# Two-layer hybrid decoder with hierarchical MoE: the last two experts' rows spread over tokens by TensorE, down weights loaded as blocks of 128 full rows

## The reference

```python
coarse_prob = softmax(xt @ wc + bc)            # 4 groups, the best one is taken
e_logit, e_idx = top_k(fine_sel, 2)            # 2 of the 4 experts of that group
e_w = softmax(e_logit) * g_prob
gate, up = split(xt @ w_gate_up[e])            # 1024 -> 2 x 256, 16 experts
y_e = (silu(gate) * up) @ w_down[e]            # 256 -> 1024
x = x + sum over the token's two experts of e_w * y_e
```

## Time and profile before

| | us |
|---|---|
| median of 3 runs (1177.66 to 1183.61) | 1181.36 |
| the profiled execution | 1181.09 |
| its span, from the first to the last instruction | 1179.3 |
| PE busy in the span | 1111.8 |
| DVE, ACT, POOL busy | 701.5, 608.6, 405.1 |

### The profile page before, as it was taken

One profiled execution on the slowest core, in us unless ns is written; L12 is line 12 of the kernel. 1 busy time (PEld: TensorE's weight loads), 2 busy tenths in 40 slices (PEclk: granted clock), 3 DMA queues, 4 the chain that ended last, 5 costly groups with the idle time before them and its releaser, 6 DMA issues.

```text
span 1179.3 us, 19724 instructions
## 1 busy us (share of the span) xinstructions
PE 1111.8 (94%) x7062; PEld 912.1 (77%) x7063; DVE 701.5 (59%) x1016; ACT 608.6 (52%) x903; POOL 405.1 (34%) x344
## 2 busy tenths in 40 slices
PE   8999999999998899998999999999999997999980
PEld 5778887778787688886788888888888886888870
DVE  5435444367736999996646341543442138999975
ACT  5556234242434699995633342233342234899871
POOL 4343121110133244442155325442244442344442
PEclk8999999999999899999999999999999997999995
DMA  9333311112225699996443213331222364999955
GB/s 262 79 86 56 72 38 55 37 44 66 72 68 210 244 353 375 379 364 238 174 128 98 81 56 106 97 106 56 81 73 91 104 190 161 354 388 374 358 208 223
DMA packets 89859, 194.76 MB, mean 165 GB/s; under 512 B 20348, under 2 KB 21432, under 8 KB 89016
## 3 DMA queue, kind: packets, MB, share of 16 engines
q1 hardware_dynamic: 67560, 159.34, 40.6%
q10 hardware_dynamic: 12432, 17.60, 4.4%
q0 software_dynamic: 9792, 16.80, 3.8%
HBM read 189.50 MB, written 23.07 MB: 180 GB/s over the span
## 4 chain that ended last, share of the span: by engine, by line
PE 80%; DVE 8%; DMA 5%; ACT 3%; issue 2%; ACTq 1%; SPq 0%; POOL 0%; POOLq 0%; DVEq 0%
PE ps L674 23%; PE ps L676 22%; PE ps L675 22%; PE ps L2570 2%; PE ps L2362 2%; DMA raw<-in_moe_w_down_dram 1%; DMA arena<-y 1%; DVE x L1467 1%; PE ps L2245 1%; ACTq L1421 1%; PE ps L2498 1%; DMA arena<-hs,slot_rows 1%; PE ps L2199 1%; ACT wh L1007 1%; DMA y<-arena,cur_rows 1%
## 5 line engine op out<-in xcount | busy, mean ns | idle before, releaser
L841 POOL TENSOR_TENSOR wl<-raw,wh 128x1024 fp32r<-128x1024 f32 x94 | 228.6, 2440 | 380.5 <-ACT wh L1007 380.2
L674 PE MATMUL ps<-wh,hT_hi 128*128 128x512 f32 x864 | 346.7, 401 | 3.5 <-DVE hT_lo L1986 2.4
L676 PE MATMUL ps<-wh,hT_lo 128*128 128x512 f32 x864 | 337.9, 391 | 0.0
L675 PE MATMUL ps<-wl,hT_hi 128*128 128x512 f32 x864 | 337.2, 390 | 0.0
L1007 ACT ACTIVATE wh<-raw 128x1024 fp32r<-128x1024 f32 x116 | 122.4, 1068 | 212.6 <-PE ps L676 191.0
L674 PEld LDWEIGHTS ps<-wh,hT_hi 128*128 128x128 f32 x864 | 162.8, 188 | 39.1 <-issue 3.5
L676 PEld LDWEIGHTS ps<-wh,hT_lo 128*128 128x128 f32 x864 | 162.3, 188 | 34.6
L675 PEld LDWEIGHTS ps<-wl,hT_hi 128*128 128x128 f32 x864 | 162.8, 188 | 30.9
L674 PE MATMUL ps<-hT_hi,wh 128*128 128x512 f32 (+1 forms) x296 | 116.9, 395 | 2.1 <-DVE arena_rounded L1818 1.0
L1961 DVE TENSOR_TENSOR wl<-arena,wh 128x1024 fp32r<-128x1024 f32 x96 | 113.8, 1222 | 4.7 <-ACT wh L1294 3.1
L1961 DVE TENSOR_TENSOR wl<-raw,wh 128x1024 fp32r<-128x1024 f32 x92 | 109.5, 1223 | 8.2 <-ACT wh L1294 5.4
(11 more groups left out here) (331 smaller groups left out, 1576.8 us busy)
## 6 DMA issues: line engine op xcount, KB each, us to landing
raw<-in_moe_w_gate_up_dram SPq DMA_DIRECT2D x64, 512.0 KB, 11.5
arena<-in_moe_w_gate_up_dram SPq DMA_DIRECT2D x64, 512.0 KB, 10.5
raw<-in_odd_w_in_dram SPq DMA_DIRECT2D x48, 512.0 KB, 3.7
raw<-in_even_w_in_dram SPq DMA_DIRECT2D x32, 512.0 KB, 4.8
arena<-in_moe_w_down_dram SPq DMA_DIRECT2D x32, 512.0 KB, 11.7
raw<-in_moe_w_down_dram SPq DMA_DIRECT2D x32, 512.0 KB, 14.1
raw<-in_odd_w_out_dram SPq DMA_DIRECT2D x16, 512.0 KB, 3.6
arena<-y ACTq DMA_DIRECT2D x6, 1024.0 KB, 9.9
```

The costliest lines, as they stand in the source:

```text
L674: nc.tensor.matmul(dst, lh, rh, start=first, stop=False)
L675: nc.tensor.matmul(dst, lh, rl, start=False, stop=False)
L676: return nc.tensor.matmul(dst, ll, rh, start=False, stop=last)
L841: pool.tensor_tensor(columns_of(i, wl[:, i % NSPL, :, :]), raw_columns(i), columns_of(i, wh[:, i % NSPL, :, :]).bitcast(F32), ALU.subtract ...
```

## The change

The last two experts of a layer, 14 and 15, are no longer scattered to DRAM. Their 128 rows each are evicted times the weight of the pair in each slot, and split into a high part (ACT, `late_hi`) and a low part (DVE, `late_low`). DVE builds for each of the two experts a matrix of zeros and ones, slot by token (`slot_tokens`), and PE multiplies it with the rows (`late_rows`): eight matmuls for each tile of 128 tokens, whose sum lands in two PSUM banks and is added to `X` by DVE (`add_late`). The weights of the slots go through DRAM: ACT stores `w12` in the turn of expert 1 and POOL gathers 128 values for each of the two experts.

The rows of the other fourteen experts are read as before, but by SP, as soon as the scatters of experts 12 and 13 have landed (`load_early_rows`), behind the four loads of block 10. A pair of experts 14 or 15 now has a row in `y2_dram` that nobody writes in this layer; its weight is set to zero (`w_early`), and the one `y2_dram`, which both layers now use, is cleared once near the start of the program from 512 zeros in SBUF.

In layer 0 the PE work without a result goes; the low parts of block 10 move from DVE to POOL, and two of its high parts stand before the eviction of expert 15 on ACT. A down piece is now a block of 128 weight rows with all 1,024 columns; so PE makes both halves of an expert's output with the first piece and then with the second, and half 0 is ready three matmuls before half 1 (`y_half`). ACT makes the next high part before both evictions instead of between them. Buffers of the rows move to other places of SBUF. The overflow part is changed to fit and isn't shown.

```diff
 def lo_by_dve(i):
-    return i in DVE_LO or any(m + 2 <= i < m + 6 * NE for m in MOE_PIECE) or first_piece(10) <= i < first_piece(10) + 4
...
+        w_dram = [nc.dram_tensor(f"w{l}", (2 * SEQ, 1), F32, kind="Internal").ap() for l in range(2)]
+        y2_dram = [nc.dram_tensor("y2", (2 * SEQ, DM), F32, kind="Internal").ap()] * 2
...
+        LAST = NE - 2
+        YP = [reg(at, 2048).rearrange("p (j d) -> p j d", j=2) for at in (0, 2048, 4096, 14336)]
+        no_rows = reg(21760, 512)
+        late_hi, late_lo = v3(rounded(9216, 2048), 2), v3(rounded(7168, 2048), 2)
...
-        def down_src(l, e, hf):
-            w = a["moe_w_down"][l].rearrange("e (k p) c -> p e k c", p=P)
-            c = 512 * hf
-            return w[:, bass.ds(e, 1), :, c:c + 512].squeeze(1) if not isinstance(e, int) else w[:, e, :, c:c + 512]
+        def down_src(l, e, k):
+            w = a["moe_w_down"][l].rearrange("e (k p) (h c) -> p e k h c", p=P, h=2)
+            return w[:, bass.ds(e, 1), k, :, :].squeeze(1) if not isinstance(e, int) else w[:, e, k, :, :]
...
+            def load_early_rows(l):
+
+                for q in range(2):
+                    sp.wait_ge(s_(f"y_stored{q}"), 112 * (l + 1))
+                src = y2_dram[l].rearrange("(T p j) d -> T p j d", p=P, j=2)
+                sp.dma_start(YP[0][:, 0, :], src[0][:, 0, :]).then_inc(s_("yp_loaded0"), 16)
+                sp.dma_start(YP[0][:, 1, :], src[0][:, 1, :]).then_inc(s_("yp_second0"), 16)
+                for T in range(1, NT):
+                    sp.dma_start(YP[T], src[T]).then_inc(s_(f"yp_loaded{T}"), 16)
...
             after = MOE_PIECE[0] + 6 * NE
             for i in range(after, after + 4):
                 load(i)
+            load_early_rows(0)
             overflow_sp(sp, 0)
-            sp.wait_ge(s_("yp_loaded3"), 16)
...
+            load_early_rows(1)
...
+                def late_experts():
+
+                    pool.wait_ge(s_("w_stored"), 16 * (l + 1))
+                    for e in range(2):
+                        rows = idx[:, 1, LAST + e:LAST + e + 1].bitcast(U32)
+                        pool.indirect_dma_start(out=w_slot[:, e:e + 1], out_offset=None, in_=w_dram[l],
+                                                in_offset=bass.IndirectOffsetOnAxis(ap=rows, axis=0),
+                                                bounds_check=last_pair_row, oob_is_err=False).then_inc(s_("late_ready"), 16)
+
                 two_experts(0)
-                with pool.Fori(1, NE // 2 - 1) as it:
+                two_experts(1)
+                late_experts()
+                with pool.Fori(2, NE // 2 - 2) as it:
                     two_experts(it)
                 for par in range(2):
-                    scatter(NE // 2 - 1, par, 32 * l + 31 + par)
-                    if par == 0:
-                        free_last(NE // 2 - 1, par)
+                    scatter(NE // 2 - 2, par, 28 * l + 27 + par)
...
                         hi_in(7)
+                    if not last:
+                        hi_in(8)
+                    if last and par == 1:
+                        hi(m + 6 * NE)
+                        hi(m + 6 * NE + 1)
                     act.wait_ge(s_("ysb_free"), E + 1)
+                    if last:
+                        act.wait_ge(s_("late_ready"), 32 * (l + 1))
                     for hf in range(2):
-                        act.wait_ge(used, it * 12 + (6 * NE * l + 6 * par + 4 + n0 + hf + 1))
-                        act.activation(ysb[:, par, 512 * hf:512 * hf + 512], ps[:, 2 + hf, :], ACT.Copy).then_inc(s_("y_read"), 1)
-                        if hf == 0 and not last:
-                            hi_in(8)
+                        c = slice(512 * hf, 512 * hf + 512)
+                        if hf == 0:
+                            act.wait_ge(s_("y_half"), E + 1)
+                        else:
+                            act.wait_ge(used, it * 12 + (6 * NE * l + 6 * par + 4 + n0 + 2))
+                        if last:
+                            act.activation(late_hi[:, par, c], ps[:, 2 + hf, :], ACT.Copy, scale=w_slot[:, par:par + 1]).then_inc(s_("y_read"), 1)
+                            continue
+                        act.activation(ysb[:, par, c], ps[:, 2 + hf, :], ACT.Copy).then_inc(s_("y_read"), 1)
 
                 for n in range(4):
                     expert(*divmod(n, 2))
+                    if n == 1:
+                        act.wait_ge(s_("w_ready"), l + 1)
+                        with nc.allow_non_contiguous_dma(reason="two weights of a token"):
+                            act.dma_start(w_dram[l].rearrange("(T p j) o -> p T (j o)", p=P, j=2), v3(w12, 4)).then_inc(s_("w_stored"), 16)
                 with act.Fori(2, NE // 2 - 1) as it:
                     for par in range(2):
                         expert(it, par)
...
-                for i in range(4):
+                for i in range(2, 4):
...
-                act.wait_ge(s_("y_all_stored"), l + 1)
-                for q in range(2):
-                    act.wait_ge(s_(f"y_stored{q}"), 128 * (l + 1))
-                src = y2_dram[l].rearrange("(T p j) d -> T p j d", p=P, j=2)
-                act.dma_start(YP[:, 0, 0, :], src[0][:, 0, :]).then_inc(s_("yp_loaded0"), 16)
-                act.dma_start(YP[:, 0, 1, :], src[0][:, 1, :]).then_inc(s_("yp_second0"), 16)
-                for T in range(1, NT):
-                    act.dma_start(YP[:, T, :, :], src[T]).then_inc(s_(f"yp_loaded{T}"), 16)
...
+                    if step[1] == 4:
+                        act.wait_ge(s_("y_cleared"), 16)
                     if not BLOCKS[step[1]][0].endswith("out"):
                         evac(step[1])
+                    if step[1] == 1:
+                        act.wait_ge(s_("no_rows_set"), 1)
+                        act.dma_start(y2_dram[0].rearrange("(p n) (k c) -> p (n k) c", p=P, c=512), no_rows.unsqueeze(1).broadcast_to([P, 16, 512]))\
+                            .then_inc(s_("y_cleared"), 16)
...
 
                 dve.wait_ge(s_("yp_second0" if T == 0 and j == 1 else f"yp_loaded{T}"), 16 * (l + 1))
-                D(stt(X[:, T, :], YP[:, T, j, :], w12[:, 2 * T + j:2 * T + j + 1], X[:, T, :], ALU.mult, ALU.add),
-                  s_(f"moe_added{l}") if j == 1 else None)
+                D(stt(X[:, T, :], YP[T][:, j, :], w_early[:, 2 * T + j:2 * T + j + 1], X[:, T, :], ALU.mult, ALU.add))
+
+            def late_low(l, e, hf):
+
+                c = slice(512 * hf, 512 * hf + 512)
+                dve.wait_ge(s_("late_ready"), 32 * (l + 1))
+                dve.wait_ge(s_("y_read"), 32 * l + 31 + 2 * e + hf)
+                stt(late_lo[:, e, c], ps[:, 2 + hf, :], w_slot[:, e:e + 1], late_hi[:, e, c].bitcast(F32), ALU.mult, ALU.subtract)\
+                    .then_inc(s_("late_low_made"), 1)
+
+            def add_late(l, T):
+
+                dve.wait_ge(s_("late_rows"), 4 * l + T + 1)
+                b = late_banks(l, T)
+                D(tt(v3(X[:, T, :], 2), v3(X[:, T, :], 2), ps[:, b:b + 2, :], ALU.add), s_(f"moe_added{l}"))
 
             def norm(n):
+                if n in (2, 4):
+                    l = n // 2 - 1
+                    combine(l, 0, 0)
+                    late_low(l, 1, 0)
+                    late_low(l, 1, 1)
+                    combine(l, 0, 1)
+                    add_late(l, 0)
+                    combine(l, 1, 0)
+                    combine(l, 1, 1)
+                    add_late(l, 1)
                 if n == 2:
-                    for i in range(4):
-                        lo(first_piece(10) + i)
-                    combine(0, 0, 0)
-                    combine(0, 0, 1)
-                    combine(0, 1, 0)
-                    combine(0, 1, 1)
                     dve.wait_ge(s_("wb_loaded"), 32)
-                    for T in range(NT):
+                    lo_tiles(("hT", n, 0), 0)
+                    for T in range(1, NT):
+                        if T + 1 < NT:
+                            combine(0, T + 1, 0)
+                            combine(0, T + 1, 1)
+                            add_late(0, T + 1)
                         lo_tiles(("hT", n, T), T)
-                        if T + 2 < NT:
-                            combine(0, T + 2, 0)
-                            combine(0, T + 2, 1)
                     return
                 if n == 4:
                     def last(T):
                         dve.wait_ge(s_("norm_r"), 16 + T + 1)
                         D(stt(fin(T), X[:, T, :], rs[:, T:T + 1], wb(4), ALU.mult, ALU.mult), s_("fin_dve"))
 
-                    for T in range(NT):
+                    dve.wait_ge(s_("wb_loaded"), 64)
+                    for T in (2, 3):
                         for j in range(2):
                             combine(1, T, j)
-                        if T == 2:
-                            dve.wait_ge(s_("wb_loaded"), 64)
-                            last(0)
-                    last(1)
+                        add_late(1, T)
```

(56 more changed lines are left out.)

100 lines of the change are left out of this document (61 added, 39 removed).

## The result

The changed kernel takes 1186.02 us (median of 8 runs, 1185.05 to 1187.07) against 1181.23 for the kernel before (8 runs as well): a ratio of 1.0045 with a 95% interval of 1.0031 to 1.0059. It is slower; 1175.2 was forecast, and the range ended at 1182. The profiled execution took 1186.38 us, its span is 1184.5 (before 1179.3).

The account below looks back on a forecast made before the run. TensorE, with 80% of the span, was taken as the bound, waiting at two seams after each layer's last expert. Terms -3.4 - 2.4 + 0.2 + 0.3 - 0.6 = -5.9 from 1181.09 gave 1175.2 us, range 1170 to 1182.

Parts of the forecast that it names:

- Splits moved: Block 10's four low parts go from VectorE to GpSimd, 9.8 us ending before block 10 starts; cost 0.
- seam 0: Stretch from layer 0's last expert to the end of block 10, where TensorE waits for rows; forecast -3.4 us.
- Weights of slots: Loops: ScalarE's store of 512 pairs, 0.4 us to issue and mostly absorbed by idle time; +0.3 for both layers.
- Down weights as full rows: Loops: larger DMA pieces save some 0.1 us an expert, buying only layer 1's 0.63 us stall; -0.6.
- Rows loaded early: Both layer ends: y loads wait for expert 13's scatter; first half tile lands in 5.7 us, VectorE starts at 547.3.
- rival (c): Rows land 2 to 3 us late behind block 10's weights, or VectorE's new operations hit upper bounds: 1179; chance 0.14.
- Slot matrices: Both layer ends: VectorE's six slot_tokens operations, between 1.4 and 4.1 us, taken as 2.2.
- Filler removed: TensorE without its resultless matmuls: one fall of the clock near 550 for about 3 us, costing 1.3.
- Rival (b): Clock stays down in seam 0, still 0.50 when block 10 starts, costing about 7.7 instead of 1.3: 1183; chance 0.11.
- Seam 1 summed: From layer 1's last expert to the end: last tile summed at 1167.4 instead of 1170.32; less 0.5 for clock, -2.4.
- Experts 14 and 15: End of each loop: TensorE's second half of expert 15 waits for expert 14's late_low, +0.1 a layer, +0.2.
- Clearing y once: Near 57 us, before the first loop: writing 4.2 MB is hidden by loads kept ahead; 0, at most some 2.

Follow-up runs that it names:

- run 9: Changed kernel with GpSimd making only 8 of the 1,024 columns of block 10's four low parts, the rest left out: 1175.65 us, ratio 0.9963.
- run 1: Changed kernel with block 10's four low parts made by VectorE again, ahead of layer 0's first combine: 1182.12 us, ratio 1.0026.
- run 2: Changed kernel with GpSimd starting block 10's low parts only once layer 0's slot matrices are complete: 1182.03 us, ratio 1.0017.
- run 5: Changed kernel with four extra 128x1024 GpSimd subtractions in layer 1, begun as VectorE begins the slot matrices; nothing uses their result: 1192.61 us, ratio 1.0090.
- run 6: Changed kernel with low parts on VectorE again and 27 filler calls (54 matmuls) on TensorE before layer 0's spreading: 1185.84 us, ratio 1.0035.
- run 10: Changed kernel with low parts on VectorE again and 13 filler calls (26 matmuls) on TensorE before layer 0's spreading: 1181.05 us, ratio 1.0004.
- run 3: Changed kernel without the store of pair weights and GpSimd's two gathers, rows of experts 14 and 15 weighted by 0.5: 1181.89 us, ratio 1.0011.
- run 7: Changed kernel with pair weights stored as one 32-byte run per partition instead of four 8-byte runs, plus five small VectorE steps: 1182.41 us, ratio 1.0010.
- run 11: Changed kernel with 32-byte weight store, low parts split up on VectorE, TensorE's products ahead of the next tile's transposes, and filler: 1179.58 us, ratio 0.9991.
- run 12: Changed kernel with 32-byte store, low parts spread on VectorE, its splits not waiting for each other, original TensorE order, filler: 1173.21 us, ratio 0.9949.
- run 4: Kernel before with the full-row down weights alone: 1180.38 us, ratio 1.0012.

## Why the prediction was wrong

The step that failed is in *Splits moved*: four low parts "from VectorE (4.6 us, hidden then) to GpSimd: 4 x 2.44 = 9.8", "Cost 0". I asked who waits for the low parts, and found nobody; I did not ask what VectorE does while GpSimd makes them. They cost seam 0 8.95 us (52.16 against 43.21 in run 9): 8.4 in the slot matrices, which took 10.6 us and not 2.2, and 0.45 in a longer wait for spread rows (1.04 against 0.59). Where VectorE makes them itself they cost 5.15 (run 1, 48.36). So neither engine makes them free any more: what had covered them was VectorE's wait for rows, and the change removes that wait. The Trainium skill, SBUF — State Buffer, "Who interferes with whom", says that a VectorE instruction with both inputs in SBUF contends with a GpSimd instruction that reads SBUF, that the pair of ports which the two engines share is an exclusive lock, and that an instruction with at most one SBUF input, outside the two-port modes, is not touched. The trace agrees: 2.27 us for 0.17 with two SBUF inputs (L2033), and 1.22 for 1.22 with one of two from PSUM (`add_late` in run 2). Two slow steps (L2032, and L2035 in run 5) have a single input from SBUF; the Trainium skill counts their form among those that can run in a two-port mode, and no run shows in which they ran. The exclusion lay in the trace of before too, in rows that the prediction does not use (a VectorE step of 64x16, twice, and GpSimd's low part of that time):

```profile
L1617 DVE SCALAR_TENSOR_TENSOR small<-small x2: 167/1266/2364, 92.2 to 92.4; 64x16 f32<-64x16 f32 x2
```

```profile
92.31 2.38 POOL L841 TENSOR_TENSOR wl<-raw,wh 128x1024 fp32r<-128x1024 f32 x1
```

The same step took 167 ns once and 2,364 ns beside a low part of 2.38 us. A group whose longest instance is fourteen times its shortest is worth a question.

The prediction named three signs of being wrong. Two came: the first combine is behind 550 (557.96), and the loop's 9.35 us an expert changed. The third, a fallen clock at block 10's start, did not.

The other steps:

- *Weights of slots*, +0.3: wrong. ScalarE's issue took 0.38, as taken, but the price is on the DMA engines: in the seven kernels with the 512 small pieces and no other edit in the loop (after, runs 1, 2, 5, 6, 9 and 10) the loops take 141.4 and 141.6 us on the mean, against 140.1 in both without them (run 3). That is 1.3 and 1.5 us, 2.8 in all; single loops of the seven lie between 140.5 and 142.6. (Why run 3's turns take 9.37 us and those of runs 7, 11 and 12 only 9.33 stays open; by the latter the store costs up to 0.5 a layer more.) I had bounded the issue from both sides and not the transfer, in a loop whose DMA share I had just read as 0.98.
- *Down weights as full rows*, -0.6: right by itself (-0.9 in run 4), but the store took the slack and the stalls came back.
- *Rows loaded early*: right. In run 9 SyncE issued the first half tile at 545.52; it landed 6.0 us later, against 5.7 in the earlier trace rows, and the combine started at 551.65, 6.1 us after the issue. The rows stood in SyncE's queue behind block 10's four loads, issued 1.7 to 5.8 us ahead of them, and landed behind them (the last load at 549.3): so far the trace agrees with the rule on ring order that the prediction cites from the Trainium skill (DMA: Bandwidth & Descriptors, "Queues, rings and completion order"). But the delay of 2 to 3 us by which rival (c) would have moved the sum is not seen: in the twelve profiles with this order the half tile took 5.5 to 7.0 us.
- *Slot matrices* 2.2, *spreading*, sums of 1.3: right; 2.2 in runs 1, 2 and 9, and `add_late` 1.22.
- *Filler removed*, 1.3: right in size, somewhat high. The clock fell to 0.50 for 13.7 us and not 3, since TensorE also waited for the slot matrices; it cost 1.0 us (runs 1 and 10), and in seam 1, where 0.5 was forecast, 0.8 between the profiles of either kind. Rival (b) had it stay down into block 10 and give 1183: the time came out on its side, but not by its mechanism, since the clock was back at 2.4 GHz before block 10 started. The rule of the Trainium skill cited there (TensorE: Matmul & The Clock Gate, Part 1) is borne out so far that TensorE without work fell to 1.2 GHz; the price is what waits for it.
- *Seam 1 summed*, -2.4: right, -2.7, and step by step (3.7 for 3.9 and 19.2 for 18.9). There GpSimd has no low parts to make.
- *Experts 14 and 15*, +0.2: right in size. The last turn of a loop takes 8.40 us in both layers, before 8.29 and 8.25; which wait makes it longer is not shown.
- +0.8 ahead of the first loop is not explained; over all the profiled runs this stretch lies between 401.2 and 405.8, so I take it for no part of the change. *Clearing y once*, taken for 0 and at most 2, falls in it: the two kernels without it took 402.7 and 401.2 (run 4), the twelve with it 401.2 to 405.8, so a cost of a microsecond is neither shown nor excluded.

The misses add up: 7.9 in seam 0 (8.95 for the low parts, less what the rest came out better), 2.9 in the loops, -0.3 in seam 1, 0.6 elsewhere: 11.1, the distance from -5.9 to +5.2.

## What to carry to other kernels

Work moved to an idle engine is not free if it keeps a busy one from its operands: before moving a tensor operation to GpSimd, list what VectorE runs at that time and which of its inputs are in SBUF; here steps of 0.17 us paid the length of a GpSimd instruction, and steps with one input from PSUM paid nothing. Where a change shortens a wait, everything that the wait had covered becomes a cost and belongs in the sum. In a stretch that moves weights at a DMA share near 1, count a store by its pieces, not by its bytes or by the issue.

## What was unexpected of the hardware

- The exclusion costs by instruction, not by size: steps of 128x8 elements took 2.26 to 2.27 us in place of 0.17, each as long as one GpSimd subtraction of 128x1024 (2.33). With long VectorE operations both sides lost: four combines lost 4.5 us and four low parts 2.9 (run 2).
- 4 KB in 512 pieces of 8 bytes took 9.7 us to land and held the loads beside it at 218 GB/s for 10 us with the DMA engines 0.89 busy, against 333 at 0.93 without it; in 128 pieces of 32 bytes it took 3.7. The loop paid 1.3 to 1.5 us for it on the mean, about 90 us later, where ScalarE came to wait for loads.
- A split of 128x128 from PSUM took 0.38 us when each waited for the one before, and 0.29 when they followed without a wait (run 12: 2.29 for eight).
